# A second linear stream's decays moved before the first one's result, and a feed-forward weight cast moved into the head

## What is computed

```
def token_mixers(u, uc, w_in, ...):
    ...
    if ctx_out:
        ...
        oc_gl, s_f, s_b = gla_bidirectional(q_gl_c, k_gl_c, v_gl_c, la_fc, la_bc, s0, s0)
    ...
    o_gl, _, _ = gla_bidirectional(to_heads(gl_q, GLA_HEADS) * GLA_DK ** -0.5, ..., la_f, la_b, s_f, s_b)

def swiglu(u, w_ffn_in, w_ffn_out):
    a, b = jnp.split(u @ w_ffn_in, 2, axis=-1)
    return (jax.nn.silu(a) * b) @ w_ffn_out
```

## Time and profile before

| | us |
|---|---|
| median of 3 runs | 2501.4 (2499.85 to 2502.88) |
| the profiled execution | 2500.61 |
| its span | 2498.8 |
| PE busy | 2295.3 (92%) |
| DVE busy | 959.1 (38%) |
| ACT busy | 637.2 (26%) |
| POOL busy | 135.8 (5%) |
| mean granted clock of PE | 0.963 |

### The profile page before, as it was taken

The page is one execution under the profiler, slowest core; times in us unless marked ns, Lnnn a source line. Parts: engine busy times, 40 slices in busy tenths (PEclk is TensorE's granted clock), DMA queues, the critical chain, the costliest instruction groups (busy, mean ns, idle before and its releaser), DMA issues. The chain is left out here.

```text
span 2498.8 us, 34079 instructions
## 1 busy us (share of the span) xinstructions
PE 2295.3 (92%) x13938; PEld 1496.6 (60%) x13938; DVE 959.1 (38%) x1773; ACT 637.2 (26%) x1028; POOL 135.8 (5%) x145
## 2 busy tenths in 40 slices
PE   6988899999999999999899877999999989888998
PEld 4866533344444344444487555678888777558997
DVE  2365321122111111211322756654344442756664
ACT  2333100011000010000332444342122252344433
POOL 0010000000000000000000232200000200211001
PEclk9989999999999999999999988999999999889999
DMA  9556899999999999999723522232332324434652
GB/s 301 169 169 202 328 406 428 428 428 428 428 429 429 428 429 428 428 429 428 283 91 131 170 90 93 83 101 70 110 101 75 101 93 140 136 118 126 181 174 93
DMA packets 264155, 606.13 MB, mean 243 GB/s; under 512 B 9808, under 2 KB 227920, under 8 KB 239344
## 3 DMA queue, kind: packets, MB, share of 16 engines
q1 hardware_dynamic: 264048, 604.61, 63.8%
HBM read 603.52 MB, written 1.05 MB: 242 GB/s over the span
## 5 line engine op out<-in xcount | busy, mean ns | idle before, releaser
L2002 PE MATMUL banks<-moe_ring,moe_x 128*64 128x512 f32 (+1 forms) x1920 | 351.2, 611 | 42.4 <-DMA moe_ring<-in_w_mlp 42.4
L2002 PEld LDWEIGHTS banks<-moe_ring,moe_x 128*64 128x64 f32 (+1 forms) x1920 | 116.7, 129 | 265.4 <-issue 264.7
L2211 DVE SCALAR_TENSOR_TENSOR res<-banks,mod,res 128x256 f32<-128x256 f32 x136 | 59.5, 479 | 519.1 <-PE banks L2023 501.2
L2562 PE MATMUL banks<-ff_xhi,ff_whi 128*128 128x512 f32 (+1 forms) x704 | 240.4, 342 | 13.6 <-DVE ff_xlo L2461 9.2
L2562 PE MATMUL banks<-ff_xhi,ff_wlo 128*128 128x512 f32 (+1 forms) x704 | 239.2, 340 | 0.0
L2562 PE MATMUL banks<-ff_xlo,ff_whi 128*128 128x512 f32 (+1 forms) x704 | 239.1, 340 | 0.0
L560 DVE TENSOR_TENSOR ff_wlo<-ring,ff_whi 128x2048 fp32r<-128x2048 f32 (+2 forms) x72 | 152.0, 2112 | 101.2 <-ACT ff_whi L551 98.9
L2104 ACT COPY moe_x<-banks 128x256 f32<-128x256 f32 x68 | 25.3, 373 | 591.3 <-PE banks L1962 591.3
L551 ACT CAST ff_whi<-ring 128x2048 fp32r<-128x2048 f32 (+2 forms) x72 | 126.4, 1756 | 124.9 <-PE banks L2594 118.4
L2562 PEld LDWEIGHTS banks<-ff_xhi,ff_whi 128*128 128x128 f32 x704 | 135.9, 193 | 31.3 <-DVE ff_wlo L560 13.9
L2562 PEld LDWEIGHTS banks<-ff_xlo,ff_whi 128*128 128x128 f32 x704 | 136.0, 193 | 13.9
(11 more groups left out here) (442 smaller groups left out, 3580.9 us busy)
## 6 DMA issues: line engine op xcount, KB each, us to landing
moe_ring<-in_w_mlp SPq DMA_DIRECT2D x128, 2048.0 KB, 17.0
ring<-in_w_mlp SPq DMA_DIRECT2D x64, 2048.0 KB, 15.7
ring<-in_w_ada SPq DMA_DIRECT2D x144, 512.0 KB, 4.6
ring<-in_w_ffn_in SPq DMA_DIRECT2D x88, 512.0 KB, 5.0
ring<-in_w_in SPq DMA_DIRECT2D x60, 512.0 KB, 4.6
ring<-in_w_out SPq DMA_DIRECT2D x24, 512.0 KB, 4.3
ring<-in_w_ffn_out SPq DMA_DIRECT2D x32, 384.0 KB, 3.1
ring<-in_w_ffn_out SPq DMA_DIRECT2D x16, 512.0 KB, 3.9
```

The costliest lines, as they stand in the source:

```text
L2002: mm = nc.tensor.matmul(u_bank[o][c:c + n_cols, :], x[:, 2 * kk + r, c:c + n_cols], self.moe_piece(2 * kk + m)[:, at:at + 512], start=Fals ...
L2211: return nc.vector.scalar_tensor_tensor(r, source, self.mod[:, 5, d, 0:1], r, ALU.mult, ALU.add)
L2562: mm = nc.tensor.matmul(bank[:, 0:width], w[:, k, :], xp[:, k, :], start=(k == 0 and term == 0), stop=(k == KC - 1 and term == 2))
```

## The change

Decays: in a stage with two streams, the second one's decays are issued in slots 14 and 15 of the first (behind the kept keys on POOL), its abs and exp passes in slots 16 and 20 of the first. The result of a stream lies in `stat` instead of `tok`. The carry, which lies in `stat` too, is made in slot 4 instead of 2, and in layer 0 waits for the first stream's end. The kept keys wait for PE's last fine products instead of DVE's last merge. Feed-forward: chunk 1 is cast in the head, before the third group, and not again behind it.

```
-    def head_scalar(self, act, head, x, width, high, high_next=None):
+    def head_scalar(self, act, head, x, width, high, high_next=None, next_at=KH):
...
-            if high_next and k0 == KH:
+            if high_next and k0 == next_at:
...
-                self.head_scalar(act, head, x, width, lambda act: self.split_high(act, bufs, n, 0))
+                self.head_scalar(act, head, x, width, lambda act: self.split_high(act, bufs, n, 0),
+                                 lambda act: self.split_high(act, bufs, n, 1), 2)
...
-                        self.split_high(act, bufs, n, at + f + 1)
+                        if part > 0 or f > 0:
+                            self.split_high(act, bufs, n, at + f + 1)
...
-            out = lambda x: tok[:, x, 0:2 * S]
+            out = lambda x: self.stat[:, x, :]
...
+                def own_decays(s, half):
+                    for i in (2 * half, 2 * half + 1):
+                        op = decays(nc.vector, s, i)
+                    if half == 1:
+                        op.then_inc(self.decay_ready.sem, self.decay_ready.one())
...
+                        if slot in (0, 1) and y == 0:
+                            own_decays(s, slot)
+                        if slot in (14, 15) and y + 1 < len(streams):
+                            own_decays(streams[y + 1], slot - 14)
...
+                def decayed(y, half):
+                    d = part(half)
+                    if half == 0:
+                        act.wait_ge(self.decay_ready.sem, self.decay_ready.at(y + 1))
+                    else:
+                        act.wait_ge(self.pool_step.sem, self.pool_step.at(y + 1))
...
+                        if slot in (2, 4) and y == 0:
+                            decayed(y, slot // 2 - 1)
+                        if slot in (16, 20) and y + 1 < len(streams):
+                            decayed(y + 1, slot // 4 - 4)
+                        if slot == 4 and s == 0:
+                            if y > 0:
+                                act.wait_ge(self.stream_done.sem, self.stream_done.at(y))
...
-                        if slot == 14 and y + 1 < len(streams):
-                            pool.wait_ge(self.fine_done.sem, self.fine_done.at(n_copies * (y + 1)))
-                            self.kept_keys(streams[y + 1], keys, k2, levels)
+                        if slot in (0, 1) and y == 0:
+                            own_decays(s, slot)
+                        if slot in (14, 15) and y + 1 < len(streams):
+                            if slot == 14:
+                                pool.wait_ge(self.sums_ready.sem, self.sums_ready.at((n_sets + 2) * (y + 1)))
+                                self.kept_keys(streams[y + 1], keys, k2, levels)
+                            own_decays(streams[y + 1], slot - 14)
```

More of the change, by code:

```diff
@@ L3169, in _ @@
             def _(act):
+                def decayed(y, half):
[4 more added lines that the diff above has]
+                        act.wait_ge(self.pool_step.sem, self.pool_step.at(y + 1))
+                    nc.scalar.activation(d, d, ACT.Abs).then_inc(self.act_step.sem, self.act_step.one())
+                    act.wait_ge(self.act_step.sem, self.act_step.count)
+                    nc.scalar.activation(d, d, ACT.Exp, scale=-1.0)\
+                        .then_inc(self.split_ready.sem, self.split_ready.one())
                 def stream(y, s):
                     for slot in range(n_stream):
[L3172 to L3182, removed]
+                        if slot in (2, 4) and y == 0:
[5 more added lines that the diff above has]
+                                act.wait_ge(self.stream_done.sem, self.stream_done.at(y))
                             for c in range(2):
@@ L3210, in _, with own_decays @@
             def _(pool):
+                def own_decays(s, half):
+                    for i in (split + 2 * half, split + 2 * half + 1):
+                        op = decays(nc.gpsimd, s, i)
+                    if half == 1:
+                        op.then_inc(self.pool_step.sem, self.pool_step.one())
                 def stream(y, s):
                     for slot in range(n_stream):
-                        if slot in (0, 1):
-                            if slot == 0 and y > 0:
-                                pool.wait_ge(self.stream_done.sem, self.stream_done.at(y))
-                            for i in (split + 2 * slot, split + 2 * slot + 1):
-                                op = decays(nc.gpsimd, s, i)
-                            if slot == 1:
-                                op.then_inc(self.pool_step.sem, self.pool_step.one())
-                        if slot == 14 and y + 1 < len(streams):
-                            pool.wait_ge(self.fine_done.sem, self.fine_done.at(n_copies * (y + 1)))
-                            self.kept_keys(streams[y + 1], keys, k2, levels)
+                        if slot in (0, 1) and y == 0:
[5 more added lines that the diff above has]
+                            own_decays(streams[y + 1], slot - 14)
                         if slot in (6, 7):
```

## The result

In the first measurement the changed kernel took 2491.97 us (median of 6 executions, 2489.61 to 2494.64) against 2501.06 before (6 executions, 2499.85 to 2502.88): ratio 0.9963, interval 0.9953 to 0.9973, so 9.1 us faster. Forecast were 2496.3 us and a range of 2492.5 to 2500.3. The direction is right, the size is not.

The account below looks back on a forecast made before the run. PE bounds the feed-forward; in the stream stage a chain running from engine to engine does. Terms 0 - 0.6 - 2.0 - 2.5 = -5.1 us from the median 2501.4 gave 2496.3 us, range 2492.5 to 2500.3.

Parts of the forecast that it names:

- Part 1, the streams: Layer 0's stream stage: earlier decays for the second stream gain nothing, since the late spread copy gives it back; 0 us.
- bounds -2.3 to +7.1: Layer 0's streams: -2.3 us if DVE and POOL take no turns, +7.1 if DVE is kept out while POOL works.
- POOL's queue decided: End of the first stream: POOL's spread copy makes PE's product 4.9 us later, DVE's own delay is only 1.7.
- the slow clock on the pair chain: PE's 4.4 us from small products to the pair's values: up to 1 us on top if slow throughout.
- Part 2, layer 0's head: Layer 0's feed-forward head: PE's 1.27 us wait goes, the third group is 0.7 late; gain 0.6 us.
- Part 2, layer 1's gap: Layer 1's feed-forward head: PE's wait for the second chunk shrinks from 3.12 to some 0.75 us; gain 2.0.
- Part 2, the slow stretch: Behind layer 1's head gap: the clock stays at 1.00 instead of 0.50 for 26 matmuls; gain 2.5 us.
- Rival A: Behind layer 1's head gap: the clock gain is absent, 2.5 us are missing, 2498.8 us; chance 0.22.
- The prediction's own signs of being wrong: Second stream's key products over 2 us sooner or later, or the clock behind layer 1's head at 0.50.
- C (DVE starved): Stream stage: POOL's ten instructions stand back to back and DVE gets no turn; slower, 2503.4 us; chance 0.08.
- B (DVE and POOL hardly disturb each other): Stream stage: the spread copy and second stream come up to 2.3 us sooner, 2494.0 us; chance 0.11.
- the half microsecond in each head delay: Both feed-forward heads: uncertainty in the third group's lateness, forecast at 0.7 us (layer 0) and 0.4 (layer 1).

Follow-up runs that it names:

- pool_after_spread: Whole change, but with POOL's four early decays behind the pair step's spread copy instead of ahead of it: 2491.45 us, ratio 0.9972.

## Why the prediction was right or wrong

**Part 1, the streams (forecast 0, bounds -2.3 to +7.1): right for layer 0.** Five profiles with this part and none of the later edits to it put the stage from 0.2 us below to 0.2 above the first profile of before. (Two more of the kernel before gave 0.1 and 2.1 below; in the latter the slow stretches lay otherwise.) POOL's queue decided, as forecast. Inside it two sizes were off and nearly cancelled. DVE's four decays took 4.56 us in all, not 7.0: the first three run beside POOL's products with one input (line 2939) and take 0.93, 0.68 and 0.88, only the fourth, beside one with two inputs, takes 2.31. The prediction let each wait for a POOL instruction and each cost POOL 0.47. POOL's kept keys took 2.33 + 9.10 = 11.43 and not 12.34: that is 9.99 and three turns of DVE, not five. So the spread copy came 1.0 sooner than forecast, and in the first profile the slow clock on the pair chain took that back, and 0.2 more, by the end of the stream. That the gains and losses came to 0 rests on two misses that offset each other.

**Part 2, layer 0's head (forecast -0.6): right in kind, -0.95.** The third group was 0.6 late, as the prediction had it (0.7), and the head's last low half started 0.2 sooner than forecast.

**Part 2, layer 1's gap (forecast -2.0): right, -2.2.** The gap is 0.65 for a forecast of 0.75; the third group is 0.3 late for 0.4. The 2.2 is the 4.7 less the 2.5 that the slow clock cost in the first profile.

**Part 2, the slow stretch (forecast -2.5): mis-sized. This step took one execution for all.** Rival A had it right that the stretch need not be there, though not as a thing that is present or absent for a kernel: behind the same gap it cost 2.5, 1.6, 2.5 and 0. Removing it is worth about 1.65 us on average.

With the terms as measured (layer 0's streams are 0.0 in the mean of their five profiles) the sum is 0 - 0.95 - 2.2 - 1.65 = -4.8, the forecast -5.1, the pooled measurement -5.9. The 1.1 us between the sum and the measurement stay open: the medians are not known better than that, and a small effect in layer 1's streams, which the prediction put at 0, would fit too. The prediction's own signs of being wrong did not come: the key products moved by 1.2 us at most, and the clock behind layer 1's head was at 1.00. C (DVE starved) did not come. B (DVE and POOL hardly disturb each other) held in part: by it the spread copy would have come up to 2.3 us before the forecast, and it came 1.0 before. C's premise is refuted by DVE's decays, which ended before the kept keys were half done.

**The step that failed is the range, and in it what the prediction gave the clock.** It allowed "some 1.5 us of its own to either side (slow clock on the pair chain, the half microsecond in each head delay)". The draw of executions had no part in that, and layer 1's streams stood in the sum at 0 with no spread. The prediction had three times of the kernel before, 2499.85 to 2502.88, looked at one slow stretch and priced it, at 2.5 us, as belonging to the change. The runs showed 2491.8 to 2504.8 us for the same kernel over 97 executions. They showed layer 1's streams between 4.3 us shorter and no longer than in the first profile with no edit at all, and 2.4 shorter in the profiled execution of the changed kernel. The slow stretch cost 0 to 2.5.

A median of 6 against a median of 6 then came out 9.1 apart, with 2491.97 us 0.5 below the range's lower end. The six of before lay at 2501.1, 1.2 above the pooled median; the six of the changed kernel at 2492.0, 2.0 below theirs. Six drawn at random from the 29 and six from the 97 differ by 9.1 us or more in about 4 of 100 draws (an estimate from these times). So it was a rare draw, and the two later measurements (4.9 and 5.8) speak for a draw. It isn't shown, though: the profiled pair of that comparison differs by 6.0 us, so the excess of 3.2 lies in the executions without a trace, and whether that comparison had something else of its own stays open. The gains of 4.9, 5.8 and, pooled, 5.9 us all lie within 1 us of the forecast of 5.1. That they lie so near is partly luck: the 0 of part 1 is the sum of two misses, and the 2.5 of the slow stretch was too much where another 1.1 us, not in the sum, came in.

## What to carry over

When a step is moved ahead in an in-order queue, follow what it is moved past: here the early decays were won and lost on one small copy behind them, and moving that copy gave some 3 us. Then ask whether the consumers were moved too: decays ready early are worth nothing while the key products still stand in their old slot behind a pair's output, and moving them gave 6 us more.

Gaps of PE cost their own length reliably, and the slow clock behind them only on average. Before a range is set for an effect of a few tenths of a per cent, ask how much the clock alone moves the same work: here most in a stage that PE shares with chains of other engines. Three times of a kernel don't tell.

## What the runs showed of the hardware

- Identical work on PE (712 matmuls in layer 1's stream stage) took between 98.0 and 103.3 us with a mean granted clock between 0.86 and 0.82 (13 profiles).
- Behind the same idle gap of 3.12 us the clock went to 0.50 for a while in three of four executions and stayed at 1.00 in one. Behind gaps of 0.65 us it stayed at 1.00 in the profile of the whole change.
- DVE and POOL on products with two inputs from SBUF take turns. A DVE subtraction of 512 columns takes 0.68 us when POOL is idle (0.47 was the prediction's working) and 1.64 each for the two at the stage's start, beside POOL's decays. The row with POOL idle, from the kernel before, whose two instructions overlap by 0.08:

```profile
1449.77 1.28 DVE L2994 TENSOR_TENSOR b_tok<-gl_near,gl_cum 128x512 f32<-128x512 f32 x2
```

- Beside POOL's kept keys with one input (line 2939) three such subtractions took 0.93, 0.68 and 0.88, little more than alone, and POOL lost one turn of 0.5 us to all three. Beside one with two inputs the fourth took 2.31, and the square took 2.70. In `pool_after_spread` DVE's product at 1505.11 took 1.36 beside POOL's decays, where the whole change's took 0.75 (at 1513.02). The Trainium skill (SBUF — State Buffer, Who interferes with whom) says that a DVE instruction with two SBUF inputs contends with a GpSimd instruction that reads SBUF, and that this contention is an exclusive lock. The rows with two inputs on both engines agree: 2.31, 2.70 and 1.36 us where the same work takes 0.68 to 0.75 without POOL. The three beside the one-input products wait less, 0 to 0.25 us.
